# Weight tiles whose k-steps are interleaved, so that TensorE reads its stationary operand at strides of 8, 2, 4 and 1 elements

## What is computed

```python
# first block, layer 0
q, k, v = split(rmsnorm(h) @ w_qkv_a); h += stick_breaking(q, k, v) @ w_o_a
h += (silu(n @ w_gate) * (n @ w_up)) @ w_down        # n = rmsnorm(h), d_ff = 2816
# first block, layer 1
k, v = split(rmsnorm(h) @ w_kv); q = rmsnorm(h) @ w_q_b
h += dilated_attention(rope(q), rope(k), v) @ w_o_b; h += swiglu(rmsnorm(h))
x = rmsnorm(h)
# second block: the mixer
proj = (rms_norm(x) * (1 + sc1) + sh1) @ w_in          # 7 x 1024 columns
y_a = (b_s * conv3(c_s * v_s)) @ w_short_out
y_b = silu(layer_norm(conv31(v_c * sigmoid(gl_c)))) @ w_conf_out
x += g1 * ((g_a * y_a + g_b * y_b) @ w_o)
# second block: its feed-forward, the "last block" below
x += g2 * ((silu(a) * b) @ w_ffn_out); return rms_norm(x)
```

## Time and profile before

| | |
|---|---|
| median of the runs | 2050.78 us (2 runs) |
| span of the profiled execution | 2050.8 us |
| time of that execution, first to last instruction | 2050.8 us |
| TensorE: stream (PE) / weight load (PEld) busy | 98% / 80% |
| VectorE / ScalarE / GpSimd busy | 52% / 39% / 31% |
| granted clock of TensorE, mean | 0.997 |
| HBM read | 211.8 MB, 104 GB/s over the span |
| matmuls, each with a weight load | 9556 |

### The profile page before, as it was taken

One profiled execution on the slowest core, in us unless ns is written; L12 is line 12 of the kernel. 1 busy time (PEld: TensorE's weight loads), 2 busy tenths in 40 slices (PEclk: granted clock), 3 DMA queues, 4 the chain that ended last, 5 costly groups with the idle time before them and its releaser, 6 DMA issues.

```text
span 2050.8 us, 28727 instructions
## 1 busy us (share of the span) xinstructions
PE 2016.6 (98%) x9556; PEld 1645.1 (80%) x9556; DVE 1066.4 (52%) x1445; ACT 798.3 (39%) x1182; POOL 629.0 (31%) x416
## 2 busy tenths in 40 slices
PE   7999999999999999999999999999999999999997
PEld 5777788888887777788888888888888888888886
DVE  6666644343465666544343456699855552332324
ACT  5545443342253444454332354222227352222224
POOL 1111255341134333246341254444444031001013
PEclk9999999999999999999999999999999999999999
DMA  4122244443234344244443332233323323333333
GB/s 155 62 72 82 83 143 166 162 144 102 92 112 93 82 84 111 77 140 174 151 146 99 95 123 73 94 101 92 102 92 93 102 83 99 95 95 100 92 102 103
DMA packets 64036, 218.80 MB, mean 107 GB/s; under 512 B 7792, under 2 KB 9968, under 8 KB 63856
## 3 DMA queue, kind: packets, MB, share of 16 engines
q1 hardware_dynamic: 60912, 213.96, 32.8%
q0 software_dynamic: 3072, 4.20, 1.6%
HBM read 211.83 MB, written 2.10 MB: 104 GB/s over the span
## 4 chain that ended last, share of the span: by engine, by line
PE 92%; DVE 3%; issue 2%; ACT 1%; POOL 1%; DMA 1%; DVEq 0%; SPq 0%; ACTq 0%; POOLq 0%
PE G L1524 28%; PE G L1526 28%; PE G L1525 28%; PE Z L1648 2%; PE O L1666 2%; PE Z L1629 2%; PE Z L1524 1%; PE Z L1526 1%; PE Z L1525 1%; DVE ez L940 0%; DVE sp L923 0%; DMA raw<-stream 0%; DVE Z L1053 0%; PE O L1675 0%; DMA qkv<-tmp 0%
## 5 line engine op out<-in xcount | busy, mean ns | idle before, releaser
L375 ACT ACTIVATE wh<-raw 128x1024 fp32r<-128x1024 f32 x338 | 358.5, 1061 | 970.0 <-PE G L1526 957.5
L1524 PE MATMUL G<-xh,wh 128*128 128x512 f32 (+1 forms) x1616 | 634.0, 392 | 10.3 <-DVE xl L835 9.5
L1525 PE MATMUL G<-xl,wh 128*128 128x512 f32 (+1 forms) x1616 | 626.9, 388 | 0.0
L1526 PE MATMUL G<-xh,wl 128*128 128x512 f32 (+1 forms) x1616 | 626.9, 388 | 0.0
L806 DVE TENSOR_TENSOR wl<-raw,wh 128x1024 fp32r<-128x1024 f32 x277 | 385.5, 1392 | 180.8 <-ACT wh L375 177.6
L1524 PEld LDWEIGHTS G<-xh,wh 128*128 128x128 f32 x1616 | 304.0, 188 | 82.8 <-issue 15.0
L1524 PE MATMUL G<-yh,wh 128*128 128x512 f32 x904 | 352.1, 389 | 3.8 <-POOL yl L1420 2.1
L1526 PEld LDWEIGHTS G<-xh,wl 128*128 128x128 f32 x1616 | 303.9, 188 | 63.3
L1525 PEld LDWEIGHTS G<-xl,wh 128*128 128x128 f32 x1616 | 304.2, 188 | 61.6 <-issue 1.0
L1526 PE MATMUL G<-yh,wl 128*128 128x512 f32 x904 | 350.6, 388 | 0.0
L1525 PE MATMUL G<-yl,wh 128*128 128x512 f32 x904 | 350.5, 388 | 0.0
(11 more groups left out here) (245 smaller groups left out, 1970.5 us busy)
## 6 DMA issues: line engine op xcount, KB each, us to landing
raw<-stream SPq DMA_DIRECT2D x340, 512.0 KB, 3.5
araw<-ada_w SPq DMA_DIRECT2D x48, 512.0 KB, 4.3
fraw<-stream SPq DMA_DIRECT2D x8, 512.0 KB, 4.7
qkv<-tmp POOLq DMA_DIRECT2D x64, 64.0 KB, 4.0
h<-x_t SPq DMA_DIRECT2D x8, 256.0 KB, 6.8
out_t<-h SPq DMA_DIRECT2D x16, 128.0 KB, 1.8
con<-const_d SPq DMA_DIRECT2D x1, 1344.0 KB, 10.3
cs<-c_row SPq DMA_DIRECT2D x1, 512.0 KB, 4.2
```

What stands on the lines that cost most here:

```text
L375: eng.activation(wh[s][:, :, :], raw[s][:, :, :], ACT.Copy).then_inc(w_hi, 1)
L1524: eng.matmul(total, hi[:, k, :], src_h[:, k, cols], start=k == 0, stop=False)
L1525: eng.matmul(total, hi[:, k, :], src_l[:, k, cols], start=False, stop=False)
L1526: mm = eng.matmul(total, lo[:, k, :], src_h[:, k, cols], start=False, stop=k == kt - 1)
```

## The change

On the host, each tile of the stream is permuted within its partition. With m taken from a table by stage, the eight k-steps are put in 8/m groups of m; inside a group, column c of its m k-steps stand side by side. Element (k, c) goes from position 128 k + c to (k // m) * 128 m + m c + k % m. The stationary operand of a matmul is then read as 128 elements that stand m apart: m is 8 in layer 0, 2 in layer 1, 4 in the mixer and 1 in the last block, where the layout is the old one. In bytes the steps are 32, 8, 16 and 4. The tiles' size, the loads, the two splitting instructions and the number and order of instructions on each engine are unchanged. The stage of a product is told by `together[0]`, which is set where the program text passes from one stage to the next; `first_unit(U_FFN[2])` has m = 1, the `joint` ahead of it m = 4.

```diff
+TOGETHER = ((U_QKV[0], 8), (U_QKV[1], 2), (U_CONF, 4), (U_FFN[2], 1))
...
+            together = [TOGETHER[0][1]]
...
                 hi, lo = (fwh[s], fwl[s]) if first else (wh[s], wl[s])
+
+                def columns_of(buf, k):
+                    m = together[0]
+                    return buf[:, :, :].rearrange("p k c -> p (k c)").rearrange(
+                        "p (a c m) -> p a c m", a=KD // m, m=m)[:, k // m, :, k % m]
...
-                    eng.matmul(total, hi[:, k, :], src_h[:, k, cols], start=k == 0, stop=False)
-                    eng.matmul(total, hi[:, k, :], src_l[:, k, cols], start=False, stop=False)
-                    mm = eng.matmul(total, lo[:, k, :], src_h[:, k, cols], start=False, stop=k == kt - 1)
+                    eng.matmul(total, columns_of(hi, k), src_h[:, k, cols], start=k == 0, stop=False)
+                    eng.matmul(total, columns_of(hi, k), src_l[:, k, cols], start=False, stop=False)
+                    mm = eng.matmul(total, columns_of(lo, k), src_h[:, k, cols], start=False, stop=k == kt - 1)
...
             ffn(0, xh, xl, yh, yl, KD, KD * (Q_FFN0 + 1))
+            together[0] = TOGETHER[1][1]
             attention(1)
...
             joint(U_CONF - 1, yh, yl, a_lo, 2 * FT - PARTS[2], PARTS[2], lambda: wide_second(O, 0))
+            together[0] = TOGETHER[2][1]
...
             joint(U_FFN[2] - 1, xh, xl, mix_lo, 0, KD, lambda: wide_square(O, 0, J_FFN, Q_FFN2))
+            together[0] = TOGETHER[3][1]
...
+    ends = [2 * u for u, _ in TOGETHER[1:]] + [2 * U_END]
+    stream = np.concatenate([
+        stream[2 * u:end].reshape(end - 2 * u, P, KD // m, m, P).transpose(0, 1, 2, 4, 3).reshape(-1, P, KD, P)
+        for (u, m), end in zip(TOGETHER, ends)])
```

## The result

The changed kernel takes 2139.55 us (median of 2 runs, 2138.43 to 2140.66) against 2050.78: a ratio of 1.0431, 95% interval 1.0412 to 1.0450. It is 89 us slower. The forecast was 2073.

What follows compares the result with a forecast made beforehand. TensorE's rhythm of matmul starts was taken as the bound. Mixer's last section 9.9, its first unit 7.7 and layer 0's returns 4.2 sum to 21.8 us on 2050.8: 2073 us, own range 2060 to 2092, 8 in 10 within 2045 to 2275.

Steps and rivals of the forecast that it cites:

- twice for 16 and 32 bytes, once for 8: Strided weight loads on TensorE: reading time doubles from 104 ns at 16 and 32 bytes, stays the same at 8.
- The mixer's last section: 96 matmuls under 256 columns at the mixer's end: starts go from 119 to 222 ns, +9.9 us.
- The first unit: Mixer's first unit, 96 matmuls under 256 columns: between +6.3 and +10.4 us, taken as +7.7 us.
- The 40 returns: Layer 0, where a product follows short matmuls: the added 104 ns is bare once per return, +4.2 us.
- layer 1 at nothing: Layer 1's 2352 loads at a step of 8 bytes read as fast as before and cost nothing.
- rival D: Layer 0 and mixer: load's reading clashes with the stream's and delays 512-column matmuls; 2100 to 2271 us; chance 0.30.
- A: All strided loads: the pattern costs nothing, loads take 104 ns at any step; 2051 us; chance 0.12.
- B: Only layer 0's step of 32 bytes pays, 4.2 us of returns remain; 2055 us; chance 0.08.
- D's second price: Layer 0 and mixer: 13.4 ns more on each of 4176 matmuls, 56 us, 2129 in all.
- C: The forecast itself: doubled loads hidden under 512 columns, bare under 256 and at returns; 2073 us; chance 0.35.
- E: Layer 0, or also the mixer: uncovered loads with three or four times the reading; 2495, 2549 or 2955 us; chance 0.12.
- F: A gain: the present clash of load and stream goes away, up to 6.5 ns on 6492 matmuls; 2009 us; chance 0.03.

Runs made afterwards that it cites:

- the matmul rows: Kernels without the network, only rows of 48 matmuls at varied steps and widths; under 256 columns 119.9 ns at step 2, 233.3 at step 4.
- the first table's kernel: Network left out, only rows of matmuls at varied steps, moving columns and number types; float32r under 512 columns 227.5 ns at step 1, 234.9 at step 4.

## Why the prediction was wrong, point by point

**Right: what bounds the kernel, and that nothing else moves.** TensorE's rhythm set the time before and after. The splits, the loads from HBM and the order cost nothing in the changed kernel, and the last block is the same to 0.1 us.

**Right in kind: twice for 16 and 32 bytes, once for 8.** PEld was forecast at 292, 188, 292 and 188 ns by stage and stands at 328, 193, 309 and 188. The added time is 140, 5, 121 and 0, against 104, 0, 104 and 0.

**Right: the places where the cover is gone.** The mixer's last section was priced at +9.9 us; it went from 12.2 (1662.6 to 1674.8) to 23.0 us (1737.6 to 1760.6), +10.8. The first unit was priced at +7.7; it takes 24.2 us (1282.54 to 1306.73) against 15.0, +9.2. The 40 returns at 104 ns each were +4.2; the chain shows 130 ns at the one above, which makes about 5.2. In all 25.2 for 21.8.

**Wrong: the step "Under 512 columns the doubled load occupies 208 ns plus the 10 by which 114 exceeds 104, that is 218 ... So 2352 + 1824 = 4176 loads just fit under their streams, and I cost them at nothing."** This is the step that failed. Its size was wrong: the load alone sets 233 ns at step 4 and 241 at step 8, both above the stream's 226.7, and under 512 columns the rhythm is 235 and 244 to 245. Its premise, that a load costs nothing until it is longer than the stream, was wrong as well, though by less: a load of 96 columns at step 8 takes 182 ns and still brings the rhythm to 237.4. At step 8 the floor of 241 gives most of the surcharge. At step 4 the floor explains 6.6 of the 8 ns, but a load that did fit would have cost about as much (233.3 ns with 64 stationary columns), so there the longer load is enough of a cause and not the only one. The stages show what that cost: of the mixer's 34.3 us, 34.3 - 10.8 - 9.2 = 14.3 are left for its 1824 matmuls, 7.8 ns each, and of layer 0's 42.3, 42.3 - 5.2 = 37.1 for its 2352, 15.8 ns each. That is 51 us where the sum had nothing, four fifths of the 64 us that the sum of 21.8 lacks of the span's 85.8.

How the size went wrong can be told. I took 0.81 ns per element from two recorded durations, of 64 and 128 columns, and doubled it: 1.62. Measured by start-to-start it is 1.74 at step 4 and 1.85 at step 8. In all the load takes 15 and 23 ns more than the 218 of the sum, and the cover had 9. I had written both ends, 218 and 228, and read "just fits" out of them; 233 lies outside. The error of my load was larger than the distance to the point where cost begins, and the term should then have been the mean over that error, not nothing.

**Wrong: layer 1 at nothing.** Its 2316 matmuls stand at 233.3 ns for 226.7, which would be 15 us; the stage lost 9.2. In the trace the steps from one product matmul to the next add up to 12.8 us more than before (in this stage they stood at 227.7 in the mean, not 226.7). 2.0 us came back behind the product, where TensorE's waits shrank, and 1.4 in attention: the granted clock was at its lower level for 6.8 us of this stage before (639.4 to 646.2), just behind a wait of 3.6 us, and for 3.4 us after (684.1 to 687.5). A 9 in a slice of the page means 90% or more and hides both. The loads of step 2 are hidden, as under 256 columns they show no loss at all (119.9 ns at both steps). So this loss is the surcharge without a long load. It has the size that rival D took from the earlier trace rows, 6.5 ns; that D's clash is its cause is not shown, and D looked for it in layer 0 and the mixer alone.

**The rivals.** A (no cost) and B (32 bytes alone) are out: 16 bytes cost as much per load as doubling. D's second price, 2129, is near the measured 2139.55, but D named the wrong cause for the larger part: the load alone sets 233 and 241 ns, since 384, 256 and 128 columns give the same rhythm at step 4 to 0.4 ns. Under 512 columns something of D's kind may be in the surcharge. The sign that I had set for D, starts 231 to 267 ns apart in layer 0 and the mixer, came true, but it does not tell D from a load that is too long; the rows over narrower streams do. What happened is C with a load that does not fit, and both signs of being wrong that stand at the end of the prediction came: a doubled load needs more than its reading and the 10 ns, and a step of 8 bytes pays. E and F did not occur.

**The pages.** By the rule cited from the Trainium skill (Advanced Engine Details and Errata, SBUF Cachelines), two hits in a line are needed, and the matmul rows agree: 8 bytes leave the load at or under 118 ns, 16 bytes double it to 233. That 8 bytes cost 6 ns under 512 columns does not follow from it. The other sentence cited from the Trainium skill (SBUF — State Buffer, Door 1: The DMA port swizzle), that four float32 elements are a free stride, does not hold for TensorE's loads: step 4 costs 113 ns per load where nothing hides it.

**What stays open.** Why step 8 is 7 ns longer than step 4 while step 16 is 11 shorter; what the surcharge of up to 10 ns under 512 columns is; and how much of the mixer's 14.3 us would be left with a load that fits. No kernel here was faster than the one before, and nothing in the rows pointed to one.

## What to carry to other kernels

Read float32r weights side by side. A step of 8 bytes cost 6 ns per matmul under a 512-column stream, 2.3% of the kernel when all stages had it, and nothing under 256 columns. From 16 bytes on the load takes twice as long and sets the rhythm itself: 4 to 8% under 512 columns, double the time under 256 or fewer. Where a forecast rests on a cover that exceeds a cost by less than the error of that cost, price the overrun, and take the cost from start-to-start times, not from recorded durations of the instruction. A load that fits under its stream is not thereby free: measure that too. A layout is paid by whoever reads it in strides: moved to the splitting instructions the same stride cost 94 us, 60 of them waits of TensorE.

## What the runs showed of the hardware that I had not expected

- A strided float32r load costs 1.74 ns per element at step 4, 1.85 at step 8, and 221 to 224 ns for 128 elements at step 16 under streams of 128 and 256 columns, so further apart is not dearer.
- Under 512 columns plain float32 (429.2 ns per record, two records per matmul) and bfloat16 (215.8) hide strided loads entirely; bfloat16 loads stay at or under 64 ns at every step up to 32 elements.
- Shifting where a 512-column moving operand starts changes the rhythm between 226.8 and 233.4 ns with nothing strided. A load of 32 or 64 columns in place of 128, also side by side, makes it slower: 231.6 and 230.0 for 227.5.
- The clock fell under long strided loads over short streams: in the first table's kernel the granted clock was at its lower level of 1.2 GHz for 7 to 14 us at a time, eight times, each beginning inside a row of 128 columns at 191 to 240 ns per start; its mean was 0.934. The strided rhythm itself did not change with it: 233.5 ns before and after the fall inside the row of step 4, 239.8 inside that of step 8. The same rows in plain float32, at 233 and 238 ns per record, kept the full clock.
- Element-wise instructions pay for a step of 32 bytes too: ScalarE 2201 ns for 1061, VectorE 2167 to 2515 for 1392, GpSimd 3078 to 3989 for 2427, on 1024 elements.
